# TensorE's filler products of two constants taken out of its pauses, in a two-layer-by-two-layer transformer block on one core

## The reference

```python
for l in range(DEPTH):
    h = rmsnorm(x, norm_mix_w[l])
    x = x + hybrid_mixer(h, w_in[l], ...)            # mLSTM, convolution, forgetting attention
    h = rmsnorm(x, norm_xattn_w[l])
    mem_n = rmsnorm(mem, norm_mem_w[l])
    x = x + memory_cross_attention(h, mem_n, ...)
    h = rmsnorm(x, norm_ffn_w[l])
    x = x + (swiglu(h, ...) if l % 2 == 0 else moe_swiglu(h, ...))   # dense, or top 2 of 8 experts
return rmsnorm(x, norm_final_w)
```

## Time and profile before

| | |
|---|---|
| device time, three executions | 2442.65 us median (2441.14 to 2442.95) |
| the profiled execution | 2438.0 us, of which the span is 2435.9 us |
| mean granted clock of TensorE | 0.981 |
| busy: TensorE (PE), VectorE (DVE), ScalarE (ACT) | 93%, 74%, 58% of the span |
| records of the filler products (L130) | 390 |

### The profile page before, as it was taken

One profiled execution on the slowest core, in us unless ns is written; L12 is line 12 of the kernel. 1 busy time (PEld: TensorE's weight loads), 2 busy tenths in 40 slices (PEclk: granted clock), 3 DMA queues, 4 the chain that ended last, 5 costly groups with the idle time before them and its releaser, 6 DMA issues.

```text
span 2435.9 us, 38979 instructions
## 1 busy us (share of the span) xinstructions
PE 2268.2 (93%) x14370; PEld 2028.2 (83%) x14370; DVE 1814.0 (74%) x2078; ACT 1414.6 (58%) x1590; POOL 71.2 (3%) x122
## 2 busy tenths in 40 slices
PE   7879999998899999988999998889999999999998
PEld 6779999877799998977899897878788887888876
DVE  5577887646778776885566688558888888888886
ACT  4456665445466664464333346437777777777775
POOL 0100000101000002000000200000000000000000
PEclk9999999999999999999999999999999999999999
DMA  7339999631299996533355652419899999999993
GB/s 252 133 116 367 394 385 354 171 107 43 100 363 383 380 369 164 197 104 121 122 189 166 160 181 92 138 38 364 330 338 391 343 356 381 336 390 338 344 394 114
DMA packets 253814, 609.46 MB, mean 250 GB/s; under 512 B 11216, under 2 KB 103200, under 8 KB 229008
## 3 DMA queue, kind: packets, MB, share of 16 engines
q1 hardware_dynamic: 247776, 590.84, 66.6%
q0 software_dynamic: 5248, 13.25, 2.4%
q10 hardware_dynamic: 560, 2.10, 0.2%
HBM read 605.11 MB, written 1.05 MB: 249 GB/s over the span
## 4 chain that ended last, share of the span: by engine, by line
PE 75%; DVE 14%; ACT 5%; issue 4%; DVEq 2%; ACTq 0%; DMA 0%; POOLq 0%
PE psum L137 16%; PE psum L139 16%; PE psum L138 16%; PE psum L2334 9%; PE psum L2367 8%; DVE weight_ring_rounded L116 2%; DVE h_cf L3294 1%; PE psum L936 1%; ACT weights_high_rounded L2423 1%; ACT scores L970 1%; ACT weights_high_rounded L2068 1%; PE psum L2875 1%; PE psum L2015 1%; PE psum L913 1%; PE psum L922 1%
## 5 line engine op out<-in xcount | busy, mean ns | idle before, releaser
L2073 DVE TENSOR_TENSOR weight_ring_rounded<-weight_ring,weights_high_rounded 128x2048 fp32r<-128x2048 f32 x264 | 603.9, 2290 | 100.9 <-ACT weights_high_rounded L2068 100.7
L2068 ACT ACTIVATE weights_high_rounded<-weight_ring 128x2048 fp32r<-128x2048 f32 x264 | 504.8, 1916 | 146.6 <-PE psum L139 132.7
L2428 DVE TENSOR_TENSOR weight_ring_rounded<-weight_ring,weights_high_rounded 128x2048 fp32r<-128x2048 f32 x128 | 292.4, 2285 | 100.8 <-ACT weights_high_rounded L2423 100.8
L137 PE MATMUL psum<-weights_high_rounded,scores_rounded 128*128 128x512 f32 (+1 forms) x768 | 291.4, 379 | 8.1 <-issue 4.3
L139 PE MATMUL psum<-weights_high_rounded,scores_rounded 128*128 128x512 f32 (+1 forms) x768 | 287.0, 374 | 0.0
L138 PE MATMUL psum<-weight_ring_rounded,scores_rounded 128*128 128x512 f32 (+1 forms) x768 | 286.5, 373 | 0.0
L2334 PE MATMUL psum<-weights_high_rounded,scores_rounded 128*128 128x256 f32 x1024 | 265.9, 297 | 7.6 <-DVE scores_rounded L2511 6.1
L2367 PE MATMUL psum<-xT_high,weight_ring 128*128 128x128 f32 x2048 | 243.4, 277 | 19.4 <-issue 18.6
L139 PE MATMUL psum<-weights_high_rounded,xT_rounded 128*128 128x512 f32 (+3 forms) x688 | 260.8, 379 | 0.0
L2367 PEld LDWEIGHTS psum<-xT_high,weight_ring 128*128 128x128 f32 x2048 | 237.1, 194 | 22.7 <-issue 21.5
L2334 PE MATMUL psum<-weight_ring_rounded,scores_rounded 128*128 128x256 f32 x1024 | 255.5, 286 | 0.0
(11 more groups left out here) (591 smaller groups left out, 4106.3 us busy)
## 6 DMA issues: line engine op xcount, KB each, us to landing
weight_ring<-in_moe_w_gate_dram SPq DMA_DIRECT2D x152, 1024.0 KB, 7.1
weight_ring<-in_moe_w_up_dram SPq DMA_DIRECT2D x152, 1024.0 KB, 9.2
weight_ring<-in_moe_w_down_dram SPq DMA_DIRECT2D x152, 1024.0 KB, 8.6
weight_ring<-in_w_in_dram SPq DMA_DIRECT2D x20, 1024.0 KB, 7.2
weight_ring<-in_ffn_w_gate_dram SPq DMA_DIRECT2D x11, 1024.0 KB, 5.3
weight_ring<-in_ffn_w_up_dram SPq DMA_DIRECT2D x11, 1024.0 KB, 5.3
weight_ring<-in_ffn_w_down_dram SPq DMA_DIRECT2D x11, 1024.0 KB, 4.9
weight_ring<-in_w_out_dram SPq DMA_DIRECT2D x8, 1024.0 KB, 5.1
```

Of the source, the lines that this page charges most:

```text
L137: nc.tensor.matmul(out, lh, rh, start=start, stop=False)
L2068: self.c.nc.scalar.activation(ring.high(self.s0 + q, 1, SLOT), ring.view(self.p0 + q, 1, SLOT), ACT.Copy).then_inc(ring.high_ready, 1)
L2073: self.c.nc.vector.tensor_tensor(ring.low(self.p0 + q, 1, SLOT), ring.view(self.p0 + q, 1, SLOT), ring.high(self.s0 + q, 1, SLOT).bitcast( ...
L2428: self.c.nc.vector.tensor_tensor(ring.low(tile, 1, SLOT), ring.view(tile, 1, SLOT), ring.high(s, 1, SLOT).bitcast(F32), ALU.subtract).then ...
```

## The change

`idle_products` returns at once, so none of its calls issues a product. No wait, no other instruction and no buffer is changed.

```diff
 def idle_products(c, pe, n, bank):
-    for _ in range(n):
-        c.nc.tensor.matmul(c.psum[:, bank, 0:TOK], c.ident[:, :], c.mask[:, :], start=True, stop=True)
+    return
```

## The result

The changed kernel took 2471.5 us as a median of four executions (2462.95 to 2474.87), the kernel before, beside it, 2442.8 us (four, 2441.14 to 2444.14). The ratio is 1.0112, 95% interval 1.0097 to 1.0127. Measured twice more, each time in six executions beside eleven of the kernel before, the same kernel stood at 1.0078 (1.0058 to 1.0098) and 1.0098 (1.0074 to 1.0122). The three agree on the direction and differ by 8 us of 2440 in the size; their mean is 1.0096, +23.5 us. The forecast was +14.0 us, 2456.7 us, with 2447 to 2468 us as its range.

A forecast was written before the change was run, and what follows sets the result against it. TensorE bounds the kernel, busy 93% of the span and 75% of the chain. Clock loss on the path 17.1 us less 3.1 us given back makes +14.0 us, 2456.7 us as a median; range 2447 to 2468 us.

The forecast's parts named there:

- thirteen long pauses: Filled TensorE pauses of 3.9 to 13 us; emptied, eleven cost 1.97 us each and two 0.6, 22.9 us of TensorE's time.
- Rival 3: The clock stands at 1.00 for another reason than the fillers; only 3.1 us come back, 2439.5 us; chance 0.05.
- rival 4: Fillers stand in the way in an in-order queue; removing them makes the kernel faster, 2437 us at 5.5 us; chance 0.03.
- the share: TensorE's 75% of the chain, taken as the part of its 22.9 us loss that is on the path: 17.1 us.
- the give-back: Six places where TensorE's next real instruction follows fillers with no idle time: 0.96, 1.04 and four of 0.28, together 3.1 us.
- nine other low stretches: Stretches at 1.2 GHz behind unfilled pauses, 4.48 us of TensorE work each, taken as the pattern for the new ones.
- the eleven short pauses: Filled pauses, 29.2 us together, priced at nothing; if six of them fell too, 11.8 us.
- rival 2: Short pauses tip too (sign: the attentions' turn low), whole loss on the path: +31.6 us, 2474 us; chance 0.10.
- 11.8 us: Upper end for the short pauses: six that lie between real products all fall, at 1.97 us each.

The follow-up runs named there:

- The light products: Kernel before with every 256-column filler replaced by two one-column products: 2487.2 us, ratio 1.0163; with one for each filler, 2466.1 us, ratio 1.0078.
- The direct test with delays: Kernel before with all fillers kept and four more products behind the wait at twelve places, 48 in all: 2454.9 us, ratio 1.0045, +10.9 us.

## Why the prediction was right in kind and too small

**The mechanism held.** The fillers were inside waits; without them the clock falls, and the work behind takes longer. L1158 took 1.97 us and takes 3.68, L621 took 3.84 and took 5.41 with its pause emptied. Low stretches stand behind all thirteen long pauses once they are empty. The light products, with which TensorE was busy for 16 of 16 us at 0.50, show that it is the clock's doing and not that of a busy queue. Rival 3 (the clock doesn't care) and rival 4 (the fillers stand in the way) are out: the mean clock is 0.957, forecast at about 0.96.

**The long pauses were sized well.** The forecast had 11 x 4.48 + 2 x 1.3 = 52 us of real work at the lower clock there, 22.9 us of TensorE's time and, with the share and the give-back, 14.0 us. With only the long pauses emptied, 58.4 us more real work lay at the lower clock, and the kernel was 14.4 us slower. The one pause emptied alone cost 1.57 us of TensorE's time, where the sum has 1.97 for each. That 14.4 meets 14.0 so closely is in part luck, as the interval is 9.8 to 19.1 us.

Two readings of the kernel before under this sum were off. The forecast speaks of one filled pause with its clock down inside; there is a second among the rows:

```profile
635.90:642.40 6.50, 5.24 (x17) 0.74 0.01 3
```

And it speaks of nine other low stretches, where the kernel before has 20, with 67.4 us of real work in them. Neither changes the sum, which counts the new stretches, but fillers didn't always keep the clock up: 11.9 us of them ran at the lower level themselves.

**The share on the path, 75%, is not refuted.** 73.7 us x 0.44 = 32.4 us of TensorE's time; the three comparisons' mean of 23.5 us is 72% of it, and 82% if the 3.1 us that the forecast gives back are added again. The direct test with delays gave 51 to 71%. It is a mean over places: all of the loss reached VectorE behind the hybrid mixer's output part, behind L621 and in the first attention, where it was followed.

**The give-back was about right where it was read.** At the norm ahead of the second hybrid mixer, the timeline of the changed kernel has VectorE's last instruction and TensorE's next:

```profile
1402.20 1.62 DVE L563 TENSOR_SCALAR probs_turned<-ident,norm_rstd 128x128 f32<-128x128 f32 x2
...
1403.90 5.49 PE L620 MATMUL psum<-probs_turned,scores 128*128 128x128 f32 x32 [10.52 <-DVEq L564]
```

1403.90 - 1403.82 = 0.08 us, against 0.96 before: 0.88 us came back, of the 0.96 in the sum. L620 then took 5.49 us in place of 3.73, and lost more. The other 2.1 us of the 3.1 in the sum were not all followed.

**The step that failed is "the eleven short pauses, 29.2 us together, I price at nothing".** Emptied alone they cost 5.9 us (1.5 to 10.0). The reason given was that six of them are short and lie between real products, that in four the clock falls anyway, and that one starts at the lower level. It doesn't hold for the two pauses of 2 us in the hybrid mixers' output part: with them empty the clock fell in the dense products behind, which cost 1.57 and 1.53 us in the profile, and 4.2 us (0.5 to 7.8) as timed. Nor does it hold for the pause that starts at the lower level, that of the first attention: its fillers took 2.2 us of the low time on themselves, and without them the attention took 2.15 us more. By the forecast's own sign for rival 2 the attentions' short pauses did turn low; its +31.6 us, with all of the loss on the path, is more than the 28.7, 19 and 24 us measured. The forecast had kept this end in the range as 11.8 us but not in the sum. 14.0 + 5.9 = 19.9 us is within the two later comparisons and below the first.

**What stays open** is the rest: some 3 us to the mean of the three comparisons, 9 to the first. The runs don't tell a further effect from the spread of the executions. How the 5.9 us divide among the eleven short pauses is open too: the attentions may carry up to 3.9 us of it, and the last layer's counting of members wasn't emptied alone.

## What to carry to other kernels

Look, for each pause of TensorE, at what runs behind it, and follow the loss in the trace: VectorE's next instructions tell whether it reached them. Price pauses of 2 us as well as those of 10: where dense work followed, a few filler products of full width ahead of it were worth some 1.5 us each time, and adding 47 in other pauses made the kernel 0.57% faster. A pause whose clock is down already is not free either, as its fillers may take the low time in place of real work. Fillers must end inside the pause; those of one column kept the clock up nowhere and held TensorE up by 5.9 us at one place. And read a difference of some us from the clocks and times of all executions, not from one pair of profiles.

## What the runs showed of the hardware that was not expected

A float32 product of one column is not cheap: its records start 0.112 us apart at the full clock, against 0.216 us for 256 columns, and 0.213 against 0.427 us at the lower one. Replacing one 256-column filler by two such made the kernel 1.6% slower. And the same products lose 44 to 45% at the lower clock, not half: 0.120 against 0.214 us at 256 columns, 0.234 against 0.427 us at 512.

The granted clock of executions of one kernel varies: 0.976 to 0.980 in 23 executions of the kernel before, with times of 2435.9 to 2452.2 us. In two profiles VectorE stood 11.3 us apart after 950 us of the same instructions.
